# First block of a split-fp32 encoder: one unit and one chunk to begin with, outputs ended one by one, small loads, squares behind the chunks

## The reference, cut to what matters

```
h = rms_norm(x, g_pre_mix[i])        # y = x * rsqrt(mean(x*x) + EPS) * g
z = h @ w_in[i]                      # columns: q_a 384 | kv_a 256 | k_rope 32 | B 512 | C 512 | conv_in 512
z_qa, z_kva, z_kr, gate_b, gate_c, conv_in = jnp.split(z, split_at, axis=-1)
```

## Time and profile before

| | us |
|---|---|
| median of 3 runs (lowest to highest) | 2876.78 (2875.25 to 2877.29) |
| the profiled execution's own time | 2878.98 |
| its span in the trace | 2877.2 |
| TensorE matmul busy | 2799.8 (97%) |
| VectorE busy | 1717.7 (60%) |
| ScalarE busy | 1203.0 (42%) |

### The profile page before, as it was taken

The page is one execution under the profiler, slowest core; times in us unless marked ns, Lnnn a source line. Parts: engine busy times, 40 slices in busy tenths (PEclk is TensorE's granted clock), DMA queues, the critical chain, the costliest instruction groups (busy, mean ns, idle before and its releaser), DMA issues.

```text
span 2877.2 us, 34913 instructions
## 1 busy us (share of the span) xinstructions
PE 2799.8 (97%) x13184; PEld 2311.0 (80%) x13184; DVE 1717.7 (60%) x2300; ACT 1203.0 (42%) x1917; POOL 113.9 (4%) x105
## 2 busy tenths in 40 slices
PE   6999999899999999999999999998999999999996
PEld 5878888688888888888887788887888888888885
DVE  4367888356544444458765588872844444444786
ACT  4336777454211211226643377773621121121473
POOL 0221000000000000000012200000000000000000
PEclk9999999999999999999999999999999999999998
DMA  4121110621111111112332111134211111111232
GB/s 149 59 74 47 32 32 23 221 91 59 51 38 57 44 44 58 44 66 96 103 108 73 56 38 32 27 106 163 82 54 40 58 44 44 58 44 44 73 103 73
DMA packets 64587, 194.93 MB, mean 68 GB/s; under 512 B 8288, under 2 KB 8288, under 8 KB 64480
## 3 DMA queue, kind: packets, MB, share of 16 engines
q1 hardware_dynamic: 64480, 193.49, 20.1%
HBM read 168.22 MB, written 25.23 MB: 67 GB/s over the span
## 4 chain that ended last, share of the span: by engine, by line
PE 93%; ACT 2%; DVE 2%; DMA 1%; issue 1%; SPq 0%; ACTq 0%; DVEq 0%
PE ps L821 28%; PE ps L823 28%; PE ps L822 28%; PE ps L988 3%; PE ps L1013 2%; PE ps L1012 2%; PE ps L1022 1%; DMA mix_lo<-yl 1%; PE ps L867 0%; PE ps L889 0%; PE ps L860 0%; ACT pth L1246 0%; DMA raw<-w_units 0%; ACT pr L1426 0%; ACT hh L1246 0%
## 5 line engine op out<-in xcount | busy, mean ns | idle before, releaser
L821 PE MATMUL ps<-hh,wh 128*128 128x512 f32 x2192 | 872.1, 398 | 25.1 <-DVE wl L1633 23.8
L823 PE MATMUL ps<-hh,wl 128*128 128x512 f32 x2192 | 856.0, 391 | 0.0
L822 PE MATMUL ps<-hl,wh 128*128 128x512 f32 x2192 | 855.9, 390 | 0.0
L821 PEld LDWEIGHTS ps<-hh,wh 128*128 128x128 f32 x2192 | 413.6, 189 | 119.7 <-issue 28.4
L822 PEld LDWEIGHTS ps<-hl,wh 128*128 128x128 f32 x2192 | 413.5, 189 | 93.5 <-issue 8.7
L823 PEld LDWEIGHTS ps<-hh,wl 128*128 128x128 f32 x2192 | 413.0, 188 | 86.7
L1246 ACT ACTIVATE wh<-raw 128x1024 fp32r<-128x1024 f32 x244 | 254.7, 1055 | 390.3 <-PE ps L823 369.8
L821 PE MATMUL ps<-gh,wh 128*128 128x512 f32 x1024 | 398.6, 389 | 0.0
L823 PE MATMUL ps<-gh,wl 128*128 128x512 f32 x1024 | 398.4, 389 | 0.0
L822 PE MATMUL ps<-gl,wh 128*128 128x512 f32 x1024 | 398.3, 389 | 0.0
L1976 DVE TENSOR_TENSOR xf<-xf,ps 128x512 f32<-128x512 f32 x464 | 310.9, 684 | 146.0 <-PE ps L823 145.5
(11 more groups left out here) (137 smaller groups left out, 3028.9 us busy)
## 6 DMA issues: line engine op xcount, KB each, us to landing
raw<-w_units SPq DMA_DIRECT2D x240, 512.0 KB, 3.3
hh<-mix_hi SPq DMA_DIRECT2D x16, 512.0 KB, 6.6
hl<-mix_lo SPq DMA_DIRECT2D x16, 512.0 KB, 7.3
stage<-w_head SPq DMA_DIRECT2D x16, 320.0 KB, 2.9
xf<-x_in SPq DMA_DIRECT2D x4, 1024.0 KB, 8.9
mix_hi<-cyh SPq DMA_DIRECT2D x8, 512.0 KB, 2.6
mix_lo<-cyl SPq DMA_DIRECT2D x8, 512.0 KB, 3.7
sq<-sums SPq DMA_DIRECT2D x32, 128.0 KB, 2.8
```

The lines of the kernel that those rows point to most:

```text
L821: nc.tensor.matmul(dst, ah, bh, start=start, stop=False)
L822: nc.tensor.matmul(dst, ah, bl, start=False, stop=False)
L823: return nc.tensor.matmul(dst, al, bh, start=False, stop=stop)
```

## The change

The first block works through its units in parts of chunks, in a written order; the constants are waited for only before the sum of squares. The first half of x comes in four pieces of 2 chunks (512 KB), by turns with the units. Units 2 and 3 go to the two halves of `bb`, a buffer not otherwise used so early, so none of these loads waits for a split; the constants come behind them. The squares of the first half follow behind all its chunks. The counts of `w_in` are lowered by one from unit 4 on, since units 2 and 3 no longer count there.

```diff
+FIRST_AT = [0, 2, 4, 6]
+        def raw_of(L, w):
+            return bb[:, w - RAW, :] if L == 0 and RAW <= w < SLOTS else raw[:, w % RAW, :]
 # SyncE
             def load_x(i):
-                t, half = i // 2, slice(i % 2 * 4, i % 2 * 4 + 4)
-                sp.dma_start(x[:, t, half, :], x_in[:, half, hs(t)]).then_inc(x_first[i], 16)
+                part = slice(2 * i, 2 * i + 2) if i < 4 else slice(4 * (i - 4), 4 * (i - 4) + 4)
+                t = i // 4
+                sp.dma_start(x[:, t, part, :], x_in[:, part, hs(t)]).then_inc(x_first[i], 16)
+            def load_beside(i):
+                sp.dma_start(bb[:, i, :], w_units[0, RAW + i]).then_inc(w_first[i], 16)
-            sp.dma_start(gv[:, :], gains[0]).then_inc(const_in, 16)
+            sp.dma_start(gv[:, :], gains[0]).then_inc(gains_first, 16)
             load(0, 0)
+            load_x(0)
             load(0, 1)
+            load_x(1)
+            load_beside(0)
+            load_x(2)
+            load_beside(1)
+            load_x(3)
             sp.dma_start(cst[:, :, :], consts).then_inc(const_in, 16)
-            load_x(0)
-            load(0, 2)
-            load(0, 3)
-            for i in range(1, 4):
-                load_x(i)
+            load_x(4)
+            load_x(5)
 # TensorE (side_by_side goes)
+            def first_part(n, part):
+                unit_ready(0, n)
+                for k in part:
+                    pe.wait_ge(pre_lo, pre_at(0, -1) * 16 + k + 1)
+                    last = split_product(ps[:, n, :], wh[:, n, k, :], wl[:, n, k, :],
+                                         hh[:, k, hs(0)], hl[:, k, hs(0)], k == 0, k == DC - 1)
+                return last
-            pe.wait_ge(const_in, 32)
                 if L == 0:
-                    for n in range(SLOTS):
-                        unit_ready(L, n)
-                    side_by_side([(n, n) for n in range(SLOTS)], 0, pre_ready(R, 0), in_out)
+                    first_part(0, range(2))
+                    first_part(1, range(2))
+                    first_part(0, range(2, 4))
+                    first_part(1, range(2, 4))
+                    first_part(2, range(4))
+                    first_part(0, range(4, DC)).then_inc(in_out, 1)
+                    first_part(1, range(4, DC)).then_inc(in_out, 1)
+                    pe.wait_ge(const_in, 16)
                     pre_stats(L, -1, 0)
+                    first_part(2, range(4, DC)).then_inc(in_out, 1)
+                    first_part(3, range(DC)).then_inc(in_out, 1)
 # ScalarE (VectorE alike: split_unit and pre_low, then all add_square)
             for c in range(DC):
-                if c % 4 == 0:
-                    split_unit(0, c // 2)
-                    split_unit(0, c // 2 + 1)
+                if c in FIRST_AT:
+                    split_unit(0, FIRST_AT.index(c))
                 if c == 0:
-                    act.wait_ge(const_in, 32)
+                    act.wait_ge(gains_first, 16)
                 pre_chunk(None, -1, 0, c)        # without its square here
+            for c in range(DC):
+                square((0, "pre", -1, 0, c), x[:, 0, c, :])
 # GpSimd, before the two pads of uu
                             pool.wait_ge(pre_lo, pre_at(L, -1) * 16 + 8)
+                            pool.wait_ge(squared, square_at(last_of(L, "pre", -1, 0)))
```

More of the change, by code:

```diff
@@ L449, in encoder @@
         stage_lo = sem("stage_lo")
-        x_first = [sem(f"x_first{i}") for i in range(4)]
+        gains_first = sem("gains_first")
+        x_first = [sem(f"x_first{i}") for i in range(6)]
+        w_first = [sem(f"w_first{i}") for i in range(2)]
         x_back = [sem(f"x_back{t}") for t in range(2)]
@@ L812, in _ @@
             for w in range(RAW):
-                sp.wait_ge(w_in[w], DEPTH * LOADS // RAW * 16)
+                sp.wait_ge(w_in[w], DEPTH * LOADS // RAW * 16 - 16)
             sp.wait_ge(mix_stored, MIX_STORED * DEPTH)
@@ L1251, in split_unit @@
                     L, w = L + 1, w - LOADS
-                act.wait_ge(w_in[w % RAW], (L * (LOADS // RAW) + w // RAW) * 16 + 16)
+                if L == 0 and RAW <= w < SLOTS:
+                    act.wait_ge(w_first[w - RAW], 16)
+                else:
+                    act.wait_ge(w_in[w % RAW], (L * (LOADS // RAW) + w // RAW - (1 if L or w >= SLOTS else 0)) * 16 + 16)
                 if L or w >= SLOTS:
                     act.wait_ge(*slot_free(L, w))
-                copy(wh[:, slot_of(w), :, :].rearrange("p k m -> p (k m)"), raw[:, w % RAW, :]).then_inc(w_hi, 1)
+                copy(wh[:, slot_of(w), :, :].rearrange("p k m -> p (k m)"), raw_of(L, w)).then_inc(w_hi, 1)
             def split_loop(L, i, g):
-                act.wait_ge(w_in[i % RAW], 32 * g + ((L * (LOADS // RAW) + (M_LOOP - 8 + i) // RAW) * 16 + 16))
+                act.wait_ge(w_in[i % RAW], 32 * g + (L * (LOADS // RAW) + (M_LOOP - 8 + i) // RAW) * 16)
                 act.wait_ge(*loop_use(L, i, g - 1))
@@ L1301, in pre_chunk @@
                 if L is None:
-                    act.wait_ge(x_first[2 * t + c // 4], 16)
+                    act.wait_ge(x_first[4 + c // 4 if t else c // 2], 16)
                 else:
@@ L1307, in pre_chunk @@
                 copy(hh[:, c, hs(t)], x[:, t, c, :], scale=gv[:, g_at + c:g_at + c + 1]).then_inc(pre_hi, 1)
+                if L is None and t == 0:
+                    return
                 e = (0, "pre", -1, t, c) if L is None else (L + 1, "pre", -1, t, c) if k == 2 else (L, "pre", k, t, c)
@@ L1638, in split_unit @@
                 dve.wait_ge(w_hi, L * LOADS + w + 1)
-                low(wl[:, slot_of(w), :, :].rearrange("p k m -> p (k m)"), raw[:, w % RAW, :],
+                low(wl[:, slot_of(w), :, :].rearrange("p k m -> p (k m)"), raw_of(L, w),
                     wh[:, slot_of(w), :, :].rearrange("p k m -> p (k m)")).then_inc(w_lo, 1)
@@ L1707, in _ @@
             for c in range(DC):
-                if c % 4 == 0:
-                    split_unit(0, c // 2)
-                    split_unit(0, c // 2 + 1)
+                if c in FIRST_AT:
+                    split_unit(0, FIRST_AT.index(c))
                 if c == 0:
-                    dve.wait_ge(const_in, 32)
+                    dve.wait_ge(gains_first, 16)
                 pre_low(None, -1, 0, c)
+            for c in range(DC):
                 add_square((0, "pre", -1, 0, c))
```

## The result

| | before | after |
|---|---|---|
| median of 4 runs, us | 2877.03 (2875.25 to 2877.38) | 2858.64 (2857.37 to 2859.83) |
| span in the trace, us | 2877.2 | 2858.0 |
| TensorE busy, us | 2799.8 (97%) | 2795.4 (98%) |

The ratio of the runs is 0.9933, 95% interval 0.992 to 0.9945: 18.4 us less. The forecast was a median of 2858.8, 18.0 us less. The kernel before has one run more here than in the table further up, so its median is 2877.03 in place of 2876.78.

A forecast was written before the change was run, and what follows sets the result against it. TensorE, busy 97%, bounds the kernel; early waits and low clock cost time. Gains of 10.85 (start), 4.77 (idle) and 2.67 (clock), less 0.3, give 18.0 us: median 2858.8, range 2856.8 to 2864.

The forecast's parts named there:

- Where the kernel loses time: TensorE, busy 97%, loses time only standing still or at low clock; two waits for units' low parts total 23.8 us.
- Start of TensorE, 8.2: First matmul at 8.2 us, once unit 0 and chunk 0 are split, against 19.05; 10.85 us earlier.
- Feed without stall: First block: units and x pieces are split in time, unit 1 with 0.2 us left; cost 0, at most 0.2.
- Squares behind: Squares after all chunks: their sum ready at 22 to 24.7, wanted at 24.4; cost 0, at the slow end 0.3.
- Sum of squares ahead of 36 matmuls: Before unit 4: 8.2 us of matmuls hide the 4.77 idle, and 2.67 of low clock in its output goes.
- Low clock in the first block: First block contains 11 low-clock matmuls' worth as before, plus 0 to 0.4 us more, taken as 0.3.
- Nothing given back later: Behind unit 4's output TensorE sets the pace, so the gain of 18.0 us carries to the end in full.
- The figure itself: Whole kernel: median forecast at 2858.8 us, 18.0 less, taken 2.2 below the profiled execution's 2861.0; chance 0.84.
- Rival 1: Unit 1's short stall prolongs the first block's low clock by 8 to 25 matmuls: 2861 to 2865; chance 0.08.
- Rival 2: First loads do not overlap, pieces taking 3.1 us each: a gain of only 5, 2872; chance 0.02.
- Rival 3: Squares come too late for the sum of squares, ready at 26.8, 2.4 late: 2861.2; chance 0.03.
- Rival 4: Gaps keep TensorE at 1.2 GHz through the first block and units 4 and 5: slower, 2885.2; chance 0.01.

The follow-up runs named there:

- e3: Changed kernel with the sum of squares moved behind the last 36 matmuls; median 2864.90 us, 13.9 less than the kernel before.
- e4: Changed kernel with each square and its add put back beside its chunk; median 2857.73 us, 21.1 less than the kernel before.
- e10: The changed kernel unaltered, run again beside others on the same chip; median 2858.22 us, 19.8 less than the kernel before.
- e12: Changed kernel with TensorE taking unit 0 over all chunks, unit 1, half of unit 2, then the sum of squares; median 2859.95 us, 18.1 less than before.
- e2: Kernel before with only TensorE's new order, its loads and ScalarE and VectorE orders old; median 2863.52 us, 15.3 less than the kernel before.
- e5: Changed kernel with the first half of x in two 1 MB pieces instead of four; median 2860.05 us, 18.1 less than the kernel before.
- e6: Changed kernel with unit 1 loaded two places later, behind x 2-3 and unit 2; median 2861.77 us, 16.4 less than the kernel before.
- e1: Changed kernel with TensorE's old order of the first block, loads staying new; median 2874.79 us, 4.1 less than the kernel before.
- e7: Changed kernel with units 0 and 1 loaded and split in two pieces, chunks 0 and 1 apart; median 2857.94 us, 20.2 less than before.
- e11: Changed kernel with units 2 and 3 loaded into the two ordinary buffers, waiting for splits; median 2858.19 us, 19.8 less than the kernel before.

## Why the prediction was right, point by point

- **Where the kernel loses time.** Right: only waits ahead of unit 5 were touched. The first went from 19.0 us to 8.4, the second, 4.8, is gone.
- **Start of TensorE, 8.2.** It was 8.39. The first x piece landed at 6.6, the slow end of the bounds, so chunk 0's high part was on the path: its low part began at 7.49, when VectorE had been free since 7.2. Four more kernels that begin with the same four loads and the same splits (e3, e4, e10, e12) started between 8.10 and 8.47.
- **Feed without stall.** Right in the trace, and the thin place was the one named: unit 1 landed at 8.4, just past my slow end of 8.3. In other traces it landed between 7.9 and 8.9, and in e3, at 8.9, TensorE waited 0.26 us for its split. So the slow end was set too low by 0.6.
- **Squares behind.** Costs nothing, as said. What it brings, at most 0.8 us (e4), the prediction did not ask. Seven adds took 5.5 us as forecast, and their sum was ready at 22.6, 1.4 before it was wanted (timeline of the changed kernel):

```profile
17.11 5.47 DVE L1688 TENSOR_TENSOR xacc<-xacc,sq 128x512 f32<-128x512 f32 x7
```

- **Sum of squares ahead of 36 matmuls.** 4.77 hidden and 2.67 of clock: e3 brings back 4.78 and 2.6. Unit 4's low part was ready at 29.8, 3.3 before TensorE wanted it; 3.4 was forecast.
- **Low clock in the first block.** Forecast 11 matmuls' worth and 0.3 us more; it came to 10 in this trace, 0.5 us less. The other traces bracket it: the first dense stretch at 0.43 lasted from 2.7 (e2, e10) to 5.7 us (e5). Where in this range a trace falls is chance.
- **Nothing given back later.** The medians say 18.4, the count up to unit 5 says 18.3. The spread behind unit 5 is wider than the difference.
- **The figure itself.** 2858.8 against 2858.64 is closer than the method allows. The start came 0.2 later and the low-clock stretch cost 0.5 less than forecast, 0.9 us came behind unit 5, and the median lay 1.2 below the profiled execution where I had taken 2.2 from the kernel before. That these cancel is luck; that the gain lies near 18 is not.
- **Rivals.** Rival 1's stall was brought about in e6: it cost its own 2.25 us, and no prolonged low clock that can be told from chance. Rival 2 is excluded by the landings, 1.2 to 1.8 us apart. Rival 3 by the sum's readiness. Rival 4 would need 90 low-clock matmuls; no trace has over 13 in the first block.

The prediction credited the loads and the order together with the early start. The runs divide it: with the old loads 14.4 of the 18.3 us come, and two parts of the change could each be left out for at most 0.8 us: the squares behind the chunks and the units loaded beside. Leaving out both at once was not tried.

## What to carry to other kernels

Let the matrix engine begin with the smallest part that has all its operands: the new loads with the old order gave 3.9 us, the new order with the old loads 14.4. Put whatever the next stage waits for (here a sum and its factor, 4.8 us) ahead of enough matmuls to hide it, since an idle stretch of this length was paid twice, once as idle time and once at the low clock (2.6 us here). Below 512 KB a piece, smaller first loads gave 1.4 us of earlier start and no time that could be measured.

## What the runs showed of the hardware

- The length of the low-clock stretch after a start is not fixed by the code: in two traces of the same kernel starts lay 0.43 apart for 4.0 us and for 2.7, and over all traces whose first stretch was dense it was 2.7 (e2) to 5.7 us (e5). At 0.20 us per matmul (0.43 against 0.23) that is over 1 us of chance in a run.
- Not every stop brings the low clock back. Behind about 4.8 us of idle time (4.77 before, 4.78 in e3, 4.8 in e1) 11 or 12 distances of 0.42 or more followed; behind stops of 0.55 and 0.90 (e12) and 1.03 (e7), in stretches at 0.23, starts were 0.23 apart again from the second to the fourth on. In the first 60 us of these traces no stop between 1.03 and 4.77 fell into a stretch at 0.23.
- The granted clock of the windows reads 1.00 over the first block although its first starts lie 0.43 apart (8.39 to 12.37 in the changed kernel); it shows the low level only from the first fall on (0.67 over unit 4's output).
- What lies behind a change can vary more than a small change brings: 2816.7 to 2820.4 us for the same program behind unit 5. Waits of TensorE for `kl` in attention came to 0.9 to 3.8 us in total, those for `sq` to 14.9 to 18.8. Why the attention stages differ from run to run stays open.
- The same loads take different times from trace to trace: with eleven loads issued behind the gains in one row, the first three took 3.3 to 4.1, 4.6 to 5.0 and 5.7 to 6.7 us from issue to landing over seven traces. With only four (e11) they took 3.4, 4.4 and 5.3, the second and third below those ranges; that is one trace, so that fewer loads behind them are the reason is seen and not shown.
